# SBUF placement of the matmul operands: one remainder of 256 bytes for all of them, and sample rows 64 columns apart

## The reference

```python
z = rms_norm(x, norm_g) @ w_in              # layer A: 1024 -> 5120 columns
...                                         # short convolution || memory attention
x = x + concat([conv_out, mem_out]) @ w_out # 1536 -> 1024
k, v = shared_kv(x, kv_norm_g, w_kv, ...)   # 1024 -> 3072, once
z = rms_norm(x, norm_g) @ w_in              # layer B: 1024 -> 3072
...                                         # banded dilated attention || memory attention
x = x + concat([dil_out, mem_out]) @ w_out  # 1024 -> 1024
```

## The kernel before

| tile | start | remainder of 256 |
|---|---|---|
| `xthi`, `xtlo` | 4896, 70432 | 32 |
| `wh0`/`wp`, `wl0`, `wh1`, `wl1` | 138304, 154688, 171072, 187456 | 64 |
| `sring` | 171072 | 64 |
| `out0_cat0`, `out0_cat1` | 138304, 203840 | 64 |
| `out1_cathi`, `out1_catlo` | 187648, 195840 | 0 |
| `a_xshl`, `b_xshl` | 137024, 136992 | 64, 32 for k = 0, and 160 bytes more for each next k |

## Time and profile before

### The profile page before, as it was taken

One profiled execution on the slowest core, in us unless ns is written; L12 is line 12 of the kernel. 1 busy time (PEld: TensorE's weight loads), 2 busy tenths in 40 slices (PEclk: granted clock), 3 DMA queues, 4 the chain that ended last, 5 costly groups with the idle time before them and its releaser, 6 DMA issues.

```text
span 2850.8 us, 38685 instructions
## 1 busy us (share of the span) xinstructions
PE 2795.3 (98%) x13662; PEld 2277.6 (80%) x13662; DVE 1757.4 (62%) x3819; ACT 1113.6 (39%) x3357; POOL 365.1 (13%) x574
## 2 busy tenths in 40 slices
PE   7999999999999999999999999999999989989999
PEld 6787878788777788878787878788787779988777
DVE  5486666758678533335565667876665756557664
ACT  5433131222326223215434353532423348756532
POOL 0001010100100000000001022323424122210000
PEclk9999999999999999999999999999999999999999
DMA  4276565555576634234266676777777788647642
GB/s 170 83 235 191 181 197 174 174 185 174 184 238 206 212 104 133 89 118 136 88 234 226 211 248 233 271 254 262 248 255 251 257 290 289 221 149 245 194 144 93
DMA packets 282873, 559.16 MB, mean 196 GB/s; under 512 B 31168, under 2 KB 81920, under 8 KB 282680
## 3 DMA queue, kind: packets, MB, share of 16 engines
q1 hardware_dynamic: 248440, 453.89, 48.8%
q0 software_dynamic: 34240, 102.80, 10.0%
HBM read 423.85 MB, written 132.72 MB: 195 GB/s over the span
## 4 chain that ended last, share of the span: by engine, by line
PE 93%; DVE 3%; DMA 2%; ACT 1%; issue 1%; SPq 0%; DVEq 0%; ACTq 0%
PE ps L130 26%; PE ps L131 26%; PE ps L132 26%; PE ps L3557 2%; PE ps L3529 2%; PE ps L3078 2%; PE ps L3062 1%; PE ps L3566 1%; PE ps L2122 1%; PE ps L3116 1%; PE ps L237 1%; PE ps L2389 1%; PE ps L3545 1%; PE ps L3540 1%; DMA tok_b_dram<-shared_o 1%; PE ps L1148 1%
## 5 line engine op out<-in xcount | busy, mean ns | idle before, releaser
L130 PE MATMUL ps<-b_wp,b_sring 128*128 128x512 f32 x640 | 249.6, 390 | 2.1 <-DMA b_sring<-sums_dram 1.0
L131 PE MATMUL ps<-b_wp,b_sring 128*128 128x512 f32 x640 | 249.1, 389 | 0.0
L132 PE MATMUL ps<-b_wp,b_sring 128*128 128x512 f32 x640 | 249.1, 389 | 0.0
L130 PE MATMUL ps<-a_sring,a_wp 128*128 128x512 f32 x512 | 199.8, 390 | 2.7 <-DMA a_sring<-sums_a_dram 2.5
L131 PE MATMUL ps<-a_sring,a_wp 128*128 128x512 f32 x512 | 199.4, 390 | 0.0
L132 PE MATMUL ps<-a_sring,a_wp 128*128 128x512 f32 x512 | 199.3, 389 | 0.0
L131 PE MATMUL ps<-b_wp,b_xthi 128*128 128x512 f32 x480 | 189.6, 395 | 0.0
L130 PE MATMUL ps<-b_wp,b_xthi 128*128 128x512 f32 x480 | 189.6, 395 | 0.0
L132 PE MATMUL ps<-b_wp,b_xtlo 128*128 128x512 f32 x480 | 189.5, 395 | 0.0
L960 DVE TENSOR_TENSOR shared_o<-ps,b_spare 128x512 f32<-128x512 f32 x160 | 109.9, 687 | 106.5 <-PE ps L132 85.5
L802 ACT ACTIVATE ps<-shared_o 128x128 f32<-128x128 f32 (+1 forms) x408 | 108.2, 265 | 157.6 <-DVE shared_o L960 149.2
(11 more groups left out here) (456 smaller groups left out, 6834.8 us busy)
## 6 DMA issues: line engine op xcount, KB each, us to landing
b_sring<-sums_dram SPq DMA_DIRECT2D x160, 512.0 KB, 5.0
a_sring<-sums_a_dram SPq DMA_DIRECT2D x128, 512.0 KB, 5.1
b_raws<-w_b_dram SPq DMA_DIRECT2D x176, 256.0 KB, 4.5
a_raws<-w_a_dram SPq DMA_DIRECT2D x140, 256.0 KB, 4.3
kv_dram<-shared_o POOLq DMA_DIRECT2D x96, 256.0 KB, 4.0
tok_b_dram<-shared_o POOLq DMA_DIRECT2D x96, 256.0 KB, 4.3
front<-tok_b_dram SPq DMA_DIRECT2D x96, 256.0 KB, 3.5
front<-grp_dram SPq DMA_DIRECT2D x48, 260.0 KB, 4.6
```

Of the source, the lines that this page charges most:

```text
L130: pe.matmul(acc, a_hi, b_hi, start=first, stop=False)
L131: pe.matmul(acc, a_hi, b_lo, start=False, stop=False)
L132: return pe.matmul(acc, a_lo, b_hi, start=False, stop=last)
```

## The change

It changes sizes and places of tiles, and four things that follow from them:

```diff
     def scores(self, st):                                   # SlabKeys: keys1_scores
-        s_t = self.core.sb(st, f"{self.tag}_scores", [P, 2, 4, H, S])
-        self.s_t = {k: s_t[:, i, 0:slabs(k), :, :] for i, k in enumerate(self.kinds)}
+        s_t = self.core.sb(st, f"{self.tag}_scores", [P, 6, H, S])
+        self.s_t = {"dil": s_t[:, 0:3, :, :], "mem": s_t[:, 3:3 + MT, :, :]}
...
-                    x = xs_hl[:, k + HK * (f in (1, 6)), :]
+                    x = xs_hl[:, k + HK * (f in (1, 6)), 0:LOW + S]
...
-        self.pr = core.sb(st, f"{tag}_pr", [HS, 3 * P + 3])
+        if self.conv:
+            self.pr = core.sb(st, f"{tag}_pr", [HS, 3 * P + 3])
...
-        core.sb(stack, "front_skip", [P, 208])
+        self.skip = core.sb(stack, "front_skip", [P, 392])
...
             x_b = core.sb(st, f"{tag}_x", [P, 2, D])
+            core.sb(st, f"{tag}_skip", [P, 16])
+            dec.pr = front.skip[0:dec.HS, 0:3 * P + 3]
...
-                core.sb(st, "a_scores", [P, 2 * 4 * H * S + 2 * 4])
-                xs_hl = core.sb(st, "a_xshl", [P, KD, LOW + S], F32R)
+                core.sb(st, "a_scores", [P, 6 * H * S])
+                xs_hl = core.sb(st, "a_xshl", [P, KD, 2 * LOW], F32R)
...
-                xs_hl = core.sb(ws, "b_xshl", [P, KD, LOW + S], F32R)
+                xs_hl = core.sb(ws, "b_xshl", [P, KD, 2 * LOW], F32R)
...
-                prep.room(ws)
+                with ExitStack() as early:
+                    core.sb(early, "b_all", [P, 4 * KD * C + 6 * D + 4 * 3 * H])
+                    prep.room(early)
```

More of the change, by code:

```diff
@@ L1196, in _ @@
                             acc_s = ps[0:LOW + S, out % 4, :]
-                            pe.matmul(acc_s, xs_hl[:, k, :], wh[b][:, k, :], start=(k == 0), stop=False)
-                            m = pe.matmul(acc_s, xs_hl[:, k, :], wl[b][:, k, :], start=False, stop=(k == KD - 1))
+                            pe.matmul(acc_s, xs_hl[:, k, 0:LOW + S], wh[b][:, k, :], start=(k == 0), stop=False)
+                            m = pe.matmul(acc_s, xs_hl[:, k, 0:LOW + S], wl[b][:, k, :], start=False, stop=(k == KD - 1))
                         else:
```

## The result

| | before | after |
|---|---|---|
| median us (4 runs each) | 2852.55 | 2820.09 |
| range us | 2851.61 to 2855.34 | 2819.84 to 2820.37 |
| ratio, 95% interval | | 0.9885 (0.9868 to 0.9902) |
| span of the profiled execution, us | 2850.8 | 2818.2 |
| PE busy in it, us | 2795.3 | 2759.3 |

The account below looks back on a forecast made before the run. PE, busy 98% of the span, was taken as the bound. Terms 41.4 - 0.8 + 1.8 = 42.4 us, at 95% 40.3, took 2852.96 to 2812.7, and 0.7 less for the median gave 2812.0 us; range 2806 to 2836.

Parts of the forecast that it names:

- rival 4: PE gets its pace, but another engine (loads, DVE's splits) takes half: 20 us lost, 2832 us; chance 0.06.
- Full operands, +41.4 us: Slow groups of lines 130 to 132: 6,240 matmuls get a difference of 0 by 256, each gaining 6.63 ns, 41.4 us.
- Sample rows, +1.8 us: 352 matmuls reading xshl: the 256-byte step puts all at 32 like wp, gaining 1.8 us, bounds 0 and 2.2.
- The sring class, 0: 3,456 sring matmuls go from 64/64 to 32/32, taken as 0; the other bound was +22.9 us.
- Rival 3: Each operand must start on a multiple of 64 bytes, so the fast class is lost: +22.9 us, 2875; chance 0.06.
- The argument from the 128x256 rows: Layer B's out stage: a 32/32 pair at 120.0 ns has the fast class's 13.3 ns overhead, so 32/32 equals 64/64.
- Memset, ACT, DVE, DMA, 0: Memset +0.2 us twice, hidden by a wait; ACT and DVE operand starts nothing; later DMA loads hidden by the ring.
- What reaches the end, 95%: 7% of the chain is not PE, so PE's gain is partly spent waiting: 40.3 of 42.4 us reaches the end.
- Rival 1: Something else than the remainder, such as same region above byte 135968, sets the class: no change, 2852; chance 0.09.
- Rival 2: The period is 512 bytes, so only cathi/catlo and xt agree: 5.1 us gained, 2847; chance 0.05.

Follow-up runs that it names:

- experiment 7: The changed kernel run once more, unaltered, as reference: 2820.44 us, ratio 0.9883 to the kernel before.
- experiment 4: Exact sweep without the computation: dense matmul streams at exact place differences by 256 bytes; at 128x512, 226.7 ns at 0, 233.3 at 32.
- experiment 6: Changed kernel with the 352 sample matmuls loading 128 columns instead of 40, xshl 256 bytes longer: 2819.49 us, ratio 0.9878 to the kernel before.
- experiment 8: Kernel of experiment 6 with 40-column sample loads again, placed at a difference of 192 from the weights: 2818.25 us, ratio 0.9880 to the kernel before.
- experiment 5: Changed kernel with both score tiles 128 bytes shorter, putting xthi and xtlo at a difference of 128: 2851.33 us, ratio 0.9986 to the kernel before.
- the sweeps: Two kernels without the computation, a first sweep with rounded places and experiment 4: dense streams at many differences, at 128x512 226.7 to 234.3 ns.

## Why the prediction was right, step by step

The mechanism was right: the pace of a dense stream depends on how the places of its two operands stand to each other, and the change makes 6,240 matmuls equal. The forecast was 2812.0, the result 2820.1, inside the range of 2806 to 2836 and just outside the forecast's own one of 2807 to 2819. 32.5 us came of 40.3, so the sum was a quarter too high, and the result lay in the range only because that reached as far as rival 4.

**Full operands, +41.4 us.** By the mean durations, in parts, with the profile of experiment 7 as the second number. The projections proper, 4,320 matmuls in the `wp`, `wh`, `prep` and `sring`-`xtlo` groups, gave 26.9 and 26.7 us against 28.6 in the sum. The out stage of A, 1,152 matmuls, gave 5.5 and 5.6 against 7.6; that of B, 768 matmuls, 2.3 and 3.3 against 5.1. The term was mis-sized by about 6 us, and 4 to 5 of them lie in the out stages. I had taken nothing off but the first matmul behind a transposition; the next five to ten aren't locked either. Summed over its 50 bursts, their distances over 226.7 ns make 1.4 us in the out stage of A; in that of B they make 1.7.

**Sample rows, +1.8 us.** The wrong sign. Their start distances, waits left out, rose from 231.3 to 232.7 ns on the average, about -0.5 us. (The mean duration of line 2122, 128 of the 352, is no guide: 406 before, 396 and 410 in two profiles of the changed kernel, by how often it was held up.) The term "352 x 5 = 1.8 us" took the rule of a 128-column load for one of 40. The bounds (0 to 2.2) didn't hold a loss. Experiments 4, 6 and 8 show where a 40-column load locks and that a 128-column one locks at 0.

**The sring class, 0.** Right: 389 to 391 before and after. Rival 3 (multiples of 64) is out, by this and by "both at 32" in experiment 4.

**The argument from the 128x256 rows.** Its conclusion was right and the reason was not, so on this point the forecast was lucky. 120.0 is what an equal remainder gives there, but unequal ones give 117.3 to 120.0, not 123 to 127. An overhead of 13.3 ns at that width doesn't tell fast from slow. Nor does the regularity of the distances: at a difference of 0 the forward pass of experiment 4 went 124, 117, 118, 121, 120 and the backward one 120, 120, 120, both with a mean of 120.0.

**Memset, ACT, DVE, DMA, 0.** The memset took 485 ns, against 520 estimated. The ACT copies stayed at 597 and 598. DVE's busy time is 1758.5 against 1757.4. Landings of `sring` loads stayed at 5.0 and 5.1 us.

**What reaches the end, 95%.** 36.0 us less busy time gave a span 32.6 us shorter: 91%. The missing 3.4 us are idle time, most of it ahead of `b_sring` matmuls, which looks like rival 4 at a tenth of its size. But the faster pace isn't shown to be its cause: experiment 5 has the old pace and the same idle time, 58.8 us against 58.9 and 59.1, and it waits 2.2 us for `b_sring`, where experiment 7 waits 1.8. There is one profile of the kernel before, so whether the new places or chance made the 3.4 us stays open.

**The other rivals.** Rival 1 (the region) is out by the sweeps, with both classes in one region, and by experiment 5. Rival 2 (a period of 512) is out too: `xt` and `wp` are 256 apart by 512 and lock. As for the rules of the Trainium skill: its page "SBUF — State Buffer" (Who interferes with whom) gives TensorE two independent read ports. Its page "TensorE: Matmul & The Clock Gate" (Back-to-back issue gap) gives a formula that makes 215.8 ns for 512 columns, which it calls the gap of an isolated matmul, and about 131 ns for a sustained stream of loads and matmuls. By either figure all the streams of experiment 4 with one shape would have had one distance. With loads of 128 columns and 512 moving ones they have 226.7 to 234.3 ns, depending on the places and, at 128 and 240, on the pass. Neither figure was seen in them. The measurement decides.

What stays open is the cause inside the chip. The runs show that the relative place, the length of the load and the width of the moving operand decide together, and that some streams can settle at one of two distances. They don't show which resource the two reads meet at.

## What to carry to other kernels

When groups of one shape and line show different means in a dense stream, compare where their operands lie before looking for a wait: here 3% of TensorE's pace hung on the remainder by 256 bytes, and could be had by filler between the tiles. The best difference holds for one shape only, so sweep it for the loads and widths that the kernel has, and read the real places of the tiles, which the allocator rounds. A locked pace needs some ten matmuls without a break; here, bursts of 12 to 36 between transpositions got only part of it.

## What the runs showed of the hardware that was not expected

- At a difference of 0 and full loads, 256, 384 and 512 moving columns have 120.0, 173.3 and 226.7 ns (granted clock 1.000). Each 128 columns add 53.3 ns, which is one column per cycle of 2.4 GHz, and 13.3 ns are left over at all three. At 128 columns it isn't so: 111.7 ns, with equal and with unequal remainders.
- For 40 loaded columns the difference that locks is 192 of 256; at 0 they have 231.8 to 232.2 ns in the sweep, and 232.7 in the kernel. Loads of 8 columns at 0 had 231.1 in one pass and 226.7 in the other.
- At 256 moving columns an equal remainder costs up to 2.7 ns more than another (120.0 against 117.3).
- Streams off zero run in patterns that repeat after a few matmuls (235, 232, 235, 231 at a difference of 32), and at 128, 192 and 240 the pattern they settle in can differ between the passes, where only the stream before is another.
